# A two-layer hybrid encoder on one core: the leading group of each feed-forward pass issues p1, p5, p2 of both pairs first, with new casts, copies and table loads around it

## The reference

```python
x = x + 0.5 * swiglu(rmsnorm(x), ...)      # ffn 0 of the layer
x = x + mixer(rmsnorm(x))                  # layer 0: conv || attention, layer 1: pooling || mLSTM
x = x + 0.5 * swiglu(rmsnorm(x), ...)      # ffn 1 of the layer

def rmsnorm(x, g):
    return x * rsqrt(mean(x * x) + EPS) * g
def swiglu(h, w_gate, w_up, w_down):       # 1024 -> 2816 -> 1024
    return (silu(h @ w_gate) * (h @ w_up)) @ w_down
```

## Time and profile before

| what | value |
|---|---|
| median of the runs | 1894.08 us (1893.21 to 1894.28) |
| profiled execution, as timed | 1894.9 us |
| its span in the trace | 1893.1 us |
| PE busy | 1834.6 us (97%) |
| DVE busy | 1356.6 us (72%) |
| ACT busy | 868.6 us (46%) |
| mean granted clock of PE | 0.989 of full |
| share of the chain that ended last | PE 85%, DVE 9%, ACT 3% |
| a split of 1024 columns: cast on ACT (L534) and difference on DVE (L1062) | 1.055 and 1.240 us |

### The profile page before, as it was taken

One profiled execution on the slowest core, in us unless ns is written; L12 is line 12 of the kernel. 1 busy time (PEld: TensorE's weight loads), 2 busy tenths in 40 slices (PEclk: granted clock), 3 DMA queues, 4 the chain that ended last, 5 costly groups with the idle time before them and its releaser, 6 DMA issues.

```text
span 1893.1 us, 31889 instructions
## 1 busy us (share of the span) xinstructions
PE 1834.6 (97%) x13095; PEld 1726.3 (91%) x13095; DVE 1356.6 (72%) x1798; ACT 868.6 (46%) x1368; POOL 53.2 (3%) x68
## 2 busy tenths in 40 slices
PE   8799999999998999999989999999999989999997
PEld 8799999999998999999979999998998879889986
DVE  7866876657777866886778678766656778668855
ACT  6443554334445543554455435544423455435542
POOL 0000000000000000000000000000123000000000
PEclk9899999999999999999999999999999999999999
DMA  7123223331222233223222323233212123333231
GB/s 187 69 87 114 90 92 103 118 122 66 68 68 73 95 95 106 90 101 101 78 78 101 98 93 101 93 114 115 79 67 68 67 68 101 97 104 101 94 113 61
DMA packets 81495, 176.81 MB, mean 93 GB/s; under 512 B 7172, under 2 KB 12580, under 8 KB 81352
## 3 DMA queue, kind: packets, MB, share of 16 engines
q1 hardware_dynamic: 80936, 174.49, 28.8%
q10 hardware_dynamic: 416, 0.29, 0.0%
HBM read 171.35 MB, written 3.41 MB: 92 GB/s over the span
## 4 chain that ended last, share of the span: by engine, by line
PE 85%; DVE 9%; ACT 3%; issue 2%; DMA 0%; SPq 0%; DVEq 0%; ACTq 0%
PE psum L1771 18%; PE psum L1830 12%; PE psum L1832 12%; PE psum L1833 12%; PE psum L1872 8%; PE psum L1781 6%; PE psum L1779 3%; PE psum L1780 3%; PE psum L1784 3%; PE psum L1783 3%; DVE rms L1196 1%; DVE wl L1062 1%; ACT fh L596 1%; DVE fl L1178 1%; ACT wh L534 1%
## 5 line engine op out<-in xcount | busy, mean ns | idle before, releaser
L1830 PE MATMUL psum<-fh,wh 128*128 128x264 f32 (+1 forms) x2016 | 590.3, 293 | 35.8 <-DVE fl L1162 19.9
L1832 PE MATMUL psum<-fl,wh 128*128 128x264 f32 (+1 forms) x2016 | 573.3, 284 | 0.0
L1833 PE MATMUL psum<-fh,wl 128*128 128x264 f32 (+1 forms) x2016 | 573.0, 284 | 0.0
L1830 PEld LDWEIGHTS psum<-fh,wh 128*128 128x128 f32 x2016 | 382.7, 190 | 41.9 <-DVE fl L1162 21.0
L1832 PEld LDWEIGHTS psum<-fl,wh 128*128 128x128 f32 x2016 | 382.2, 190 | 2.7
L1833 PEld LDWEIGHTS psum<-fh,wl 128*128 128x128 f32 x2016 | 382.1, 190 | 0.0
L1062 DVE TENSOR_TENSOR wl<-raw,wh 128x1024 fp32r<-128x1024 f32 x189 | 233.2, 1240 | 152.4 <-ACT wh L534 152.3
L534 ACT ACTIVATE wh<-raw 128x1024 fp32r<-128x1024 f32 x190 | 199.5, 1055 | 273.7 <-PE psum L1771 160.2
L1771 PE MATMUL psum<-xs,wh 128*128 128x264 f32 (+1 forms) x1120 | 204.5, 301 | 4.6 <-DVE xs L1149 3.4
L1781 PE MATMUL psum<-hs,wh 128*128 128x512 f32 x528 | 208.3, 395 | 0.0
L1771 PE MATMUL psum<-hs,wh 128*128 128x512 f32 (+2 forms) x760 | 192.5, 349 | 0.8 <-DVE hs L1281 0.8
(11 more groups left out here) (303 smaller groups left out, 2861.0 us busy)
## 6 DMA issues: line engine op xcount, KB each, us to landing
raw<-in_w_gate_up SPq DMA_DIRECT2D x175, 512.0 KB, 3.6
raw<-in_w_down SPq DMA_DIRECT2D x64, 384.0 KB, 3.2
raw<-in_w_down SPq DMA_DIRECT2D x64, 320.0 KB, 2.9
raw<-in_od_in SPq DMA_DIRECT2D x21, 512.0 KB, 3.5
raw<-in_ev_in SPq DMA_DIRECT2D x18, 512.0 KB, 3.5
raw<-in_ev_out SPq DMA_DIRECT2D x8, 512.0 KB, 3.5
raw<-in_od_out SPq DMA_DIRECT2D x8, 512.0 KB, 3.4
x<-in_x_t SPq DMA_DIRECT2D x8, 264.0 KB, 5.0
```

The costliest lines, as they stand in the source:

```text
L1830: pe.matmul(psum[:, bank, 0:w], wh[:, slot, cols], high_x, start=start and j == 0, stop=False, skip_group_check=True)
L1832: pe.matmul(psum[:, bank, 0:w], wh[:, slot, cols], low_x, start=False, stop=False, skip_group_check=True)
L1833: last = pe.matmul(psum[:, bank, 0:w], wl[:, slot, cols], high_x, start=False, stop=j == 3, skip_group_check=True)
```

## The change

In the leading group of every pass PE now runs p1(n), p5(n), p1(n+1), p5(n+1), p2(n), p2(n+1), [sums of squares], p7(n), p6(n), p7(n+1), p6(n+1), p3(n), p4(n). p5 no longer lies on top of u: it starts its own bank, and VectorE takes u from that bank in `c22`, by one more instruction of 264 columns for each n. The forms are regrouped: B11 and T1 are "first" (`first_forms`, `first_low`, two forms each, plus a negative copy of T1), the other four follow. The s1 of a leading group takes the place that s3 had, and s3 that of s1. In a pass (q, 0) with q > 0 the sums of squares go straight from float32 by two matmuls (`pair_sums`) into the banks of the two p7, so p7(n) waits for the root. The casts of the last tile's other forms stand behind the first `p1_copy`. Two one-column activations (`warm`) bring the function tables of Sqrt and of Silu ahead. On VectorE `low_a22`, `low_a11` and `sum_s3` of the next group stand ahead of the first c22, and the reciprocal behind it. The std stage of block 0 is written out in a new order; the low-part half of each of its accumulators is copied out by ScalarE (`std_rest`).

```diff
@@ ScalarE, groups
                     p1_copy(2 * g, real)
+                    if g == first:
+                        if q and not p:
+                            other_forms(q, 3, real)
+                        p1_copy(2 * g + 1, real)
+                        if (q, p) == (0, 0):
+                            high_s4(g)
+                        high_a22(g)
+                        if q and not p:
+                            pair_root(V_FFN[q], real)
+                            warm(ACT.Silu)
+                        high_a11(g + 1)
...
@@ ScalarE, std stage of block 0, up to the first root
+            for m in ORDER[0:3]:
+                gained(0, m, False)
+            first_forms(0, 0, False)
+            first_forms(0, 1, False)
+            high(4)
+            for m in ORDER[3:6]:
+                gained(0, m, False)
+            first_forms(0, 2, False)
+            high(5)
+            root(0)
...
@@ VectorE, x_tile
+            def first_low(q, j, real):
+                w = width(real)
+                dve.wait_ge(first_high, 4 * q + j + 1)
+                dve.wait_ge(t1_negative, 4 * q + j + 1)
+                dve.tensor_tensor(fl[:, B11:T1 + 1:2, j, 0:w], ff[:, B11:T1 + 1:2, j, 0:w], f32(fh[:, 0:2, j, 0:w]),
+                                  ALU.subtract).then_inc(first_ready, 1)
@@ VectorE, c22
+                    dve.tensor_tensor(bank, bank, u, ALU.subtract).then_inc(u_added, 1)
+                    dve.wait_ge(u_added, added)
@@ VectorE, groups
+                    if g == first:
+                        if (q, p) == (0, 0):
+                            low_s4(g)
+                        low_a22(g)
+                        low_a11(g + 1)
+                        sum_s3(g + 1)
                     c22(2 * g, real)
                     if g == first and q and not p:
                         norm(V_FFN[q], real)
                     if g > first:
                         low_a22(g)
-                    if g + 1 < end:
+                    if g > first and g + 1 < end:
                         low_a11(g + 1)
                         sum_s3(g + 1)
                     gate_a_out(g, real)
@@ PE, ffn, leading group
                         p1(n, real, new)
-                        if q == 3 and p == 0:
-                            fresh(n + 1, 2)
-                            pe.matmul(psum[:, 5, 0:BACK], wh[:, 4, 0:P], fh[:, 0, 0, 0:BACK], start=True, stop=True)
+                        p5(n, real, new)
                         p1(n + 1, real, new)
+                        p5(n + 1, real, new)
+                        p2(n, real, new)
+                        p2(n + 1, real, new)
+                        if q and not p:
+                            pair_sums(V_FFN[q], real)
                         p7(n, real, new)
                         p6(n, real, new)
-                        if q and not p:
-                            pe.wait_ge(acc_free, tiles_before(TILE[down_name(q, p)], 3))
-                            sums(V_FFN[q], 3, real)
-                        p2(n, real)
-                        p5(n, real)
-                        if q and not p:
-                            pe.wait_ge(root_ready, V_FFN[q] + 1)
-                        p7(n + 1, real)
+                        p7(n + 1, real, new)
+                        p6(n + 1, real, new)
                         p3(n, real)
-                        p6(n + 1, real)
                         p4(n, real)
-                        p2(n + 1, real)
-                        p5(n + 1, real)
                         continue
```

More of the change, by code:

```diff
@@ L80, in raw_slot, with leads, leading, ring_place @@
     return (CHUNK[down_name(*PASS_OF[g])] + QUARTERS.index(kind)) % RING
-def form_slot(kind, g):
-    if kind in RING_FORMS:
-        return (CHUNK[down_name(*PASS_OF[g])] + RING_FORMS.index(kind)) % RING
-    return 4 if kind == "a11" else 5
+def leads(g):
+    return g == GROUP[PASS_OF[g]][0]
+def leading(g):
+    return sum(leads(h) for h in range(g + 1))
+def ring_place(kind, g):
+    return RING_FORMS.index("s1" if leads(g) and kind == "s3" else kind)
+def form_slot(kind, g):
+    if kind == "a11":
+        return 4
+    if kind == ("s1" if leads(g) else "s3"):
+        return 5
+    return (CHUNK[down_name(*PASS_OF[g])] + ring_place(kind, g)) % RING
 RAW_COUNT, RAW_BEFORE = {}, {}
@@ L796, in _, with std_rest @@
             high_sum(0)
-            for f in range(STD_F):
-                if f < 2:
-                    high(2 * f + 4)
-                if f == 0:
-                    root(0)
-                if f < 2:
-                    high(2 * f + 5)
-                if f == 2:
-                    act.wait_ge(table_out, 16)
-                    high_a11(0)
-                    high_s3(0)
+            def std_rest(c):
+                act.wait_ge(chunk_done, c + 1)
+                act.activation(spare[:, 1 + c % 2, 0:BACK], back(c % 4, 1), ACT.Copy).then_inc(std_back, 1)
@@ new lines, in _ @@
+            high(6)
+            for m in ORDER[6:8]:
+                gained(0, m, False)
+            first_forms(0, 3, False)
+            std_rest(2)
+            std_silu(1)
+            std_rest(3)
+            high(7)
+            std_hidden(1)
+            act.wait_ge(table_out, 16)
+            high_a11(0)
+            high_s1(0)
+            std_rest(4)
+            std_silu(2)
+            other_forms(0, 0, False)
+            std_rest(5)
+            high_s2(0)
+            std_hidden(2)
@@ L1338, in down @@
                         next_low(n + 2 * i)
+                        if g is not None and i == 5:
+                            low_a11(g)
                         next_low(n + 2 * i + 1)
@@ L1341, in down @@
                         sum_s1(g)
+                        sum_s3(g)
                         sum_s2(g)
+                        low_s1(g)
+                    elif i == 7 and g is not None:
+                        low_s2(g)
                         low_s3(g)
-                        low_s2(g)
-                    elif i == 7 and g is not None:
                         sum_s4(g)
+                        low_s4(g)
                     dve.wait_ge(chunk_done, n + 2 * i + 2)
@@ L1360, in down @@
                         x_tile(q + 1, i, False)
-                    if g is not None and i == 5:
-                        low_a11(g)
-                        sum_s3(g)
-                    if g is not None and i == 6:
-                        low_s1(g)
-                    if g is not None and i == 7:
-                        low_s4(g)
-                        low_a22(g)
-                if p and not last:
+                if ring_next:
                     low_sum(V_FFN[q] + 1)
@@ L1820, in free, with pair_sums @@
                     pe.wait_ge(acc_free, tiles_before(tile))
+            def pair_sums(v, real):
+                t = TILE[down_name(PASS_OF_V[v], 0)]
+                pe.wait_ge(acc_free, tiles_before(t, 1))
+                pe.wait_ge(acc_free, tiles_before(t, 3))
+                pe.wait_ge(ss_ready, KT * (v + 1))
+                lo, w = (N_META, BACK) if real else (0, HALF)
+                for h in range(2):
+                    last = pe.matmul(psum[:, 4 * h + 3, 0:w], ones[:, :], ss[:, lo + w * h:lo + w * (h + 1)], start=True, stop=True)
+                last.then_inc(stat_done, 1)
             def product(weights, slot, s, x_form, bank, start, real, q=None):
```

370 lines of the change are left out of this document (210 added, 160 removed).

## The result

The kernel after takes **1910.07 us** in the median of 4 runs (1908.32 to 1915.82) against 1894.18 (1893.21 to 1895.15) for the kernel before on the same chip: ratio 1.0089, 95% interval 1.0067 to 1.0111. The predicted time was 1905, the range 1897 to 1914: slower as forecast, by 15.9 us where 11.3 had been worked out. A second series of the same kernel gave 1915.09 (1910.95 to 1915.94), ratio 1.011 (1.0094 to 1.0127). Over both, the kernel after spreads over 7.6 us, the kernel before over 2 to 4.5 in each series. That spread turns out to be part of the answer. The median lies inside the stated range, but outside the 1898.5 to 1909 that had been given to the forecast itself.

A forecast was written before the change was run, and what follows sets the result against it. PE, busy 97% of the span, was taken as the bound, so time could be won only where it idles or clocks lower. Terms 8.0 - 1.9 + 0.1 + 5.1 = +11.3 us on 1894.1 gave about 1905, range 1897 to 1914.

The forecast's parts named there:

- Step 1: End of the leading group, all eight passes: PE waits 2.0 us for c21; unrecovered in four (q, 1) passes, +8.0 us.
- Step 2: Start of pass (1, 0): DVE and ACT bound it, most waits come back elsewhere; c21 ends at 601.0, gain 0.8 us.
- Step 3: Starts of passes (2, 0) and (3, 0): same working as in (1, 0), gains of 0.5 and 0.8 us.
- Step 4: Block 0, std stage and pass (0, 0): late root stalls PE 5.9 us at no cost; +0.1 us in all, least certain.
- Step 5: PE's clock: one low stretch each in blocks 0 and 2, one in blocks 1 or 3, 3 x 1.7 = +5.1 us.
- The third rival: Slower still: 1.9 us waits lower the clock in half the passes or more, 4 to 5 x 1.7 more, 1912; chance 0.18.
- The cover works: Faster: p1, p5 and p2 cover the waits for forms at (q, 0) starts, -15 us, 1879; chance 0.07.
- The rival of a drain behind each table load: ScalarE idles 1.4 us behind each table load in the chain, giving 1913; chance 0.02.

The follow-up runs named there:

- the seven executions above: Profiled executions with eight c21 waits of 1.85 to 2.22 us: two of the kernel after, five with loads, s4 cast, reciprocal, root or p1 copies moved.
- the fastest kernel: Kernel after plus s1 and table loads early, gain first, block 0's p1 copies early, (q, 0) work on VectorE and ScalarE reordered: 1877.76 us, ratio 0.9905 to before.

## Why the prediction was right, step by step

The range was met and the direction too. The mechanism of steps 1 to 4 was right; the term of step 5, the clock, was half of what it should have been, and a part of the surplus was given back elsewhere by luck.

**Step 1, the end of the leading group (+8.0).** Right, in mechanism and size. Eight waits of 1.85 to 2.2 us ended by c21; the four of (q, 1) add 9.8 us, of which 1.4 is one stretch of low clock, so 8.4. Three kernels take the wait away or shorten it, from VectorE's side by one and by two instructions and from PE's side by one product, and each moves it by the amount of the working.

**Step 2, pass (1, 0) (-0.8).** The chain was followed to half a microsecond. The trace after lies 3.4 us later from the pass before it; less that, here is each step as forecast and as found: gain 580.4 and 580.6, p2(n) 582.05 and 582.2, p7(n) behind the root 587.4 and 587.9, `gate_a_out` 596.4 and 596.7, end of c21 601.0 and 601.3. The five waits of the working were 2.1, 2.3, 0.9, 1.0 and 2.4. PE in that stretch (the second row is from a view that ends at 588, and counts 11 of the 16 matmuls of the two p2):

```profile
578.51 0.39 PE L1955 MATMUL psum<-fh,wh 128*128 128x264 f32 x1 [1.72 <-DVE fl L1253]
585.61 2.69 PE L2002 MATMUL psum<-ff,raw 128*128 128x264 f32 x11 [2.08 <-issue]
591.29 0.36 PE L1955 MATMUL psum<-fh,wh 128*128 128x264 f32 x1 [0.99 <-ACT rms L655]
600.95 0.36 PE L1955 MATMUL psum<-fh,wh 128*128 128x264 f32 x1 [0.69 <-DVE gate L1353]
604.82 0.44 PE L1955 MATMUL psum<-fh,wh 128*128 128x264 f32 x1 [2.15 <-DVE spare L1349]
```

The first two and the last are up to 0.4 shorter than forecast, the fourth 0.3. The start won 0.5 where 0.8 was forecast.

**Step 3, (2, 0) and (3, 0) (-0.5 and -0.8).** (3, 0) won 0.4. (2, 0) did not win but lost 1.9 to the end of c21 (983.59 against 974.97, a shift of 8.6, where it was about 6.7 in the stage ahead). Its place is known: p2(n) started at 962.34, less 6.7 that is 955.6 (forecast 955.5), but the two p2 and the sums took 7.87 us to p7(n), where in (1, 0) they took 5.68. The window shows why (length, busy times, PEclk 0.57, DMA):

```profile
959.00:967.00 8.00, 4.66 (x11) 3.72 (x12) 5.70 (x9) 3.89 (x7) 0.00 (x0) 0.57 0.18 71
```

That is the clock of step 5: a double stretch, 3.4 us of work, of which 2.2 came into the chain.

**Step 4, block 0 (+0.1).** Measured +1.3, of which 1.8 is the stretch of low clock behind the wait ahead of p2(n) that step 5 had counted; without it -0.5. The root ended at 33.97 (forecast 34.7), PE stood 5.70 us ahead of c3 (5.9), p2(n) started at 75.56 after 4.71 (76.3 after 5), the next p7 at 93.09 (92.0). The claim that the late root costs nothing is shown by the kernel with an early one. What did cost was the copy of p1 behind the last cast, and that was named.

**Step 5, the clock (+5.1).** This term was mis-sized. Time lost to low clock in the stretches that count: 1.8 in block 0, 2.2 in the chain of (2, 0), and 1.4 behind each of four c21 waits, in (1, 0), (1, 1), (2, 0) and (3, 0): 9.7 us in the profiled execution, where 3 x 1.7 had been put. The stretches expected in blocks 0 and 2 came; the one behind 2.3 or 2.4 us of idle time did not. What the sum left out were the waits of 1.9 us of step 1: it let them pass without a price and left them to a rival with 0.18. In the seven executions above 35 of 56 were followed by a stretch, so five of eight, 7 us.

The working also read two rows of the kernel before too loosely. Of the waits of 3.1 and 4.3 us only the second was followed by low clock; behind the first the granted clock stayed at 1.00 from 576 to 584. And in block 0 the low clock began at 62.4, ahead of the 7.67 us wait and not behind it.

**The sum.** The starts of the passes add 16.7 us against 11.3: 9.7 against 5.1 for the clock, 7.0 against 6.2 for the rest. The stages between gave 3.3 back, which the working did not have; that the profiled execution ends at 13.4, nearer to the forecast, is luck.

**The spread.** The runs of the kernel after over both series span 1908.3 to 1915.9. Their mean granted clocks are 0.989 for the fastest and 0.985 for the slowest four, and 0.004 of 1910 us is 7.6 us of work: the low clock makes most of the spread.

**The third rival.** It said 4 to 5 stretches behind the waits of 1.9 us, and 1912. That is what happened: four in the profiled execution, five in the next, and a median nearer to 1912 than to 1905 (1910.07 and 1915.09). It deserved more than 0.18.

**The rivals.** *The cover works* fell as the text had it: p2(n) waited for ACT in all four blocks (4.7, 2.1, 5.4 and 0.9 us). But the fastest kernel shows that its conditions could be made, and then the gain is as large as that rival's (-18 against -15). The rival of a drain behind each table load is not there: in the kernel after, every activation that waits for nothing but the load starts 0.01 us behind it.

**A sum that misleads.** The clock record gives 17.1 us of work lost to low clock before and 17.1 after (without the last 10 us of the launch, where PE has nearly nothing to do). The sum tells nothing. Of the 17.1 before, 6.8 lie in one long stretch around the waits of block 0, where PE waited for forms anyway. That the other stretches before also lay beside the chain, and those after in it, is my reading; no run separates it.

## What to carry to other kernels

Before moving products forward, measure for each bank the distance between the product that lets VectorE start and the product that needs the bank back, against VectorE's row of work between. Products taken out of that distance are paid for as idle time. If the new order is wanted, move VectorE's independent instructions (here one or two sums) out of that row into its idle time ahead of it. And give each new wait of about 2 us on TensorE a price for low clock too: behind the c21 waits here it was 0.6 x 1.4 us on average. A wait need not go altogether for that: cut to 0.6 to 0.9 us, none of eight was followed by a stretch.

## What the runs showed of the hardware

- Low clock (1.2 GHz in place of 2.4) follows waits shorter than most of the earlier trace rows: behind 1.85 to 2.22 us of idle PE, ended by c21, in 35 of 56 cases (0.62), and behind none of the eight of 0.59 to 0.94 us. The length alone doesn't decide it. Six waits of 1.8 to 1.9 us (three each in the kernels with p3 or s1 moved) and nine of 2.1 to 2.2 us ahead of p2 were followed by none. All three waits of 3.1 us in the kernel with both sums moved were (the third from within it), but the one of 3.1 us in the kernel before was not. What else decides, these runs don't tell.
- Each such stretch takes 1.7 us of work by the clock record, or twice that; the one in block 0 of the kernel before, four times that. In time it costs less behind c21, 1.4 us, and 1.8 in the two p2 of block 0.
- The same kernel has more or fewer of them from one execution to the next. Its runs spread over 7.6 us, where those of the fastest kernel, whose c21 waits are 0.9 to 1.5 us and which has three stretches in the whole span ahead of the last 10 us, spread over 2.0.
